# Two fp32-split feed-forwards on one core: high and low halves of the activations in one moving operand, and earlier norm diagonals

## The reference

```
# first block
h = rmsnorm(x, norm_mix_g);  proj = h @ w_in          # then RG-LRU, mLSTM, stick-breaking attention
x = x + merged @ w_o
hf = rmsnorm(x, norm_ffn_g)
gate, up = split(hf @ w_ffn_in)                        # 1024 -> 2 x 2816
x = x + (silu(gate) * up) @ w_ffn_out                  # 2816 -> 1024
x = rmsnorm(x, final_norm_g)
# second block
h = rms_norm(x, pre_mix_g)                             # mixer: spatial gating, MoBA attention, conv
x = x + rms_norm(concat(ya, yb, yc) @ w_out, post_mix_g)
m = rms_norm(mem, mem_g)                               # cross-attention on 256 memory tokens, w_xq, w_xkv, w_xo
h = rms_norm(x, pre_ffn_g)
f = square(relu(h @ w_ff1)) @ w_ff2                    # 1024 -> 4096 -> 1024
x = x + rms_norm(f, post_ffn_g)
```

## Time and profile before

| | us |
|---|---|
| median of three runs | 799.4 |
| lowest, highest | 798.67, 800.1 |
| the profiled execution, whole | 800.34 |
| its span in the profile | 798.6 |

### The profile page before, as it was taken

The page is one execution under the profiler, slowest core; times in us unless marked ns, Lnnn a source line. Parts: engine busy times, 40 slices in busy tenths (PEclk is TensorE's granted clock), DMA queues, the critical chain, the costliest instruction groups (busy, mean ns, idle before and its releaser), DMA issues.

```text
span 798.6 us, 11574 instructions
## 1 busy us (share of the span) xinstructions
PE 773.1 (97%) x4939; PEld 700.4 (88%) x4939; DVE 488.8 (61%) x528; ACT 387.9 (49%) x474; POOL 74.7 (9%) x87
## 2 busy tenths in 40 slices
PE   8999999989999999999969999999999999999996
PEld 8989887868999999999969888789988999999995
DVE  4555955486665556555655999776546655455543
ACT  6277466543553344343533478556345444444341
POOL 2000004020000000000214233020002000000001
PEclk9999999999999999999989999999999999999999
DMA  8455463436465654665534544446324655555431
GB/s 294 133 194 209 135 234 112 179 132 211 131 206 192 195 174 158 192 215 179 190 122 160 158 158 159 158 158 238 105 93 137 204 186 199 181 189 174 161 140 53
DMA packets 73940, 135.73 MB, mean 170 GB/s; under 512 B 4363, under 2 KB 28833, under 8 KB 73889
## 3 DMA queue, kind: packets, MB, share of 16 engines
q1 hardware_dynamic: 72080, 130.80, 49.0%
q10 hardware_dynamic: 1808, 4.19, 1.6%
HBM read 133.93 MB, written 1.05 MB: 169 GB/s over the span
## 4 chain that ended last, share of the span: by engine, by line
PE 89%; DVE 4%; ACT 3%; issue 1%; POOL 1%; DMA 0%; ACTq 0%; DVEq 0%
PE bank L1720 88%; DVE low L1175 2%; ACT arena L672 1%; PE bank L1807 1%; ACT high L672 1%; POOL arena L595 1%; ACT xn L672 0%; DVE arena L1376 0%; DMA vec_rows<-in_norm_mix_g_dram 0%; DVE x L1545 0%; ACT act_h L672 0%; DVE act_l L1224 0%; DVE arena L1467 0%; DVE arena L1358 0%; POOL var L524 0%
## 5 line engine op out<-in xcount | busy, mean ns | idle before, releaser
L1175 DVE TENSOR_TENSOR low<-raw,high 128x2048 fp32r<-128x2048 f32 (+1 forms) x118 | 266.2, 2279 | 142.0 <-ACT high L672 141.1
L672 ACT ACTIVATE high<-raw 128x2048 fp32r<-128x2048 f32 (+1 forms) x124 | 233.9, 1899 | 143.1 <-PE bank L1720 140.6
L1720 PE MATMUL bank<-act_h,low 128*128 128x256 f32 x864 | 246.5, 285 | 3.0 <-DVE act_l L1224 3.0
L1720 PE MATMUL bank<-act_h,high 128*128 128x256 f32 x864 | 245.7, 284 | 0.0
L1720 PE MATMUL bank<-act_l,high 128*128 128x256 f32 x864 | 245.6, 284 | 0.0
L1720 PEld LDWEIGHTS bank<-act_h,low 128*128 128x128 f32 x864 | 166.7, 193 | 4.2 <-issue 3.4
L1720 PEld LDWEIGHTS bank<-act_l,high 128*128 128x128 f32 x864 | 166.6, 193 | 0.7
L1720 PEld LDWEIGHTS bank<-act_h,high 128*128 128x128 f32 x864 | 166.6, 193 | 0.0
L1720 PE MATMUL bank<-high,act_l 128*128 128x512 f32 (+1 forms) x264 | 103.0, 390 | 2.8 <-DVE arena L1376 1.6
L1720 PE MATMUL bank<-high,hid_l 128*128 128x512 f32 x264 | 103.7, 393 | 0.0
L1720 PE MATMUL bank<-low,hid_h 128*128 128x512 f32 x264 | 103.0, 390 | 0.0
(11 more groups left out here) (180 smaller groups left out, 669.6 us busy)
## 6 DMA issues: line engine op xcount, KB each, us to landing
raw<-in_w_ff_dram SPq DMA_DIRECT2D x32, 1024.0 KB, 5.3
raw<-in_w_in_dram SPq DMA_DIRECT2D x30, 1024.0 KB, 5.4
raw<-in_w_ffn_in_dram SPq DMA_DIRECT2D x44, 512.0 KB, 4.8
raw<-in_w_ffn_out_dram SPq DMA_DIRECT2D x11, 1024.0 KB, 6.6
raw<-in_w_xkv_dram SPq DMA_DIRECT2D x8, 1024.0 KB, 5.1
raw<-in_w_o_dram SPq DMA_DIRECT2D x4, 1024.0 KB, 5.1
raw<-in_w_out_dram SPq DMA_DIRECT2D x4, 1024.0 KB, 5.1
raw<-in_w_xq_dram SPq DMA_DIRECT2D x4, 1024.0 KB, 5.1
```

The source lines that it names most:

```text
L672: return act.activation(dst, src, func, **k)
L1175: tt(part(low, g), part(raw, g), f32(part(high, g)), SUB).then_inc(sem.low_by_dve, 1)
L1720: return pe.matmul(dst, lhs, rhs, start=start, stop=stop, skip_group_check=loose)
```

## The change

`act_h` and `act_l` become one tile `act_hl` [128, 4, 2, 512], in which for each pair of row tiles the 512 numbers of the high part stand ahead of the 512 of the low part. For a row tile the high and the low 256 columns can be taken as one moving operand of two pieces (`both_of`).

A new mode "S" is used for the up products of both feed-forwards from c = 2 on. For a row tile and a channel tile it issues two matmuls: high weights by both halves of x, 512 columns, into a whole bank, and low weights by the high half, 256 columns, into the first half of the bank. So a chunk uses all four banks 0 to 3, which are now one PSUM tensor `wide`. ScalarE copies the second halves of the banks to SBUF (`hidden_low`, two copies of 512 columns that read two banks each), VectorE adds the first halves (`hidden_sum`, twice), and the chains go on from the sums; in the second feed-forward the ReLU becomes part of VectorE's multiply. TensorE waits for both sums of the chunk before (`hid_sum`) ahead of an up product.

At the seam VectorE makes the diagonals of norm 2 before `ahead_of(("kv", 0), "C")` and only the low quarters behind it, and ScalarE's `norm_split(2)` waits for one kv group less.

```
             if is_mem:
                 return hid_h[kt // 4][:, kt % 4, :], hid_l[kt // 4][:, kt % 4, :]
-            return act_h[:, kt, :], act_l[:, kt, :]
+            k = slice(kt % 2 * T, (kt % 2 + 1) * T)
+            return act_hl[:, kt // 2, 0, k], act_hl[:, kt // 2, 1, k]
+        def both_of(kt):
+            return act_hl[:, kt // 2, :, kt % 2 * T:(kt % 2 + 1) * T]
+        def wide_of(b, low_part):
+            return wide[:, 2 * b:2 * b + 2, low_part * T:(low_part + 1) * T]
...
-                self.pairs += {"W": 2, "F": 0}.get(mode, 1)
+                self.pairs += {"W": 2, "S": 2, "F": 0}.get(mode, 1)
...          # ScalarE
-                        act.wait_ge(sem.w_used, me.used - (n == 4))
+                        act.wait_ge(sem.w_used, me.used - (n in (2, 4)))
...
+            def hidden_low():
+                act.wait_ge(sem.w_used, me.used)
+                for b in range(2):
+                    f(in2(h_low[b]), wide_of(b, 1), ACT.Copy).then_inc(sem.hid_low, 1)
             def hidden1(c):
+                if c >= 2:
+                    hidden_low()
                 act.wait_ge(sem.hid_g, me.seen("hid_g"))
...
             def hidden2(c):
+                if c >= 2:
+                    hidden_low()
+                    for b in range(2):
+                        act.wait_ge(sem.hid_a, me.seen("hid_a", 1))
+                        f(flat(hid_h[c % 2][:, 2 * b:2 * b + 2, :]), (h_val, h_tmp)[b], ACT.Copy).then_inc(sem.hid_h, 1)
+                    return
...          # VectorE
+            def hidden_sum(b):
+                dve.wait_ge(sem.hid_low, me.seen("hid_low"))
+                tt(in2(h_low[b]), wide_of(b, 0), in2(h_low[b]), ADD).then_inc(sem.hid_sum, 1)
+                dve.wait_ge(sem.hid_sum, me.seen("hid_sum"))
             def hidden1(c):
-                dve.wait_ge(sem.w_used, me.used)
-                b0, b1 = me.pair()
-                tt(in2(h_tmp), in2(b0[:, :]), rep_2(), MUL).then_inc(sem.hid_g, 1)
+                if c >= 2:
+                    hidden_sum(0)
+                    gate, up = h_low
+                else:
+                    dve.wait_ge(sem.w_used, me.used)
+                    gate, up = (b[:, :] for b in me.pair())
+                tt(in2(h_tmp), in2(gate), rep_2(), MUL).then_inc(sem.hid_g, 1)
+                if c >= 2:
+                    hidden_sum(1)
                 dve.wait_ge(sem.hid_t, me.seen("hid_t"))
...
             def hidden2(c):
+                if c >= 2:
+                    value = h_val, h_tmp
+                    for b in range(2):
+                        hidden_sum(b)
+                    for b in range(2):
+                        stt(value[b], h_low[b], 0.0, h_low[b], MAX, MUL).then_inc(sem.hid_a, 1)
+                    for b in range(2):
+                        dve.wait_ge(sem.hid_h, me.seen("hid_h"))
+                        hl = flat(hid_l[c % 2][:, 2 * b:2 * b + 2, :])
+                        tt(hl, value[b], f32(flat(hid_h[c % 2][:, 2 * b:2 * b + 2, :])), SUB).then_inc(sem.hid_hl, 1)
+                        dve.wait_ge(sem.hid_hl, me.seen("hid_hl"))
+                    return
...
             final_norm()
+            norm_diag(2)
             ahead_of(("kv", 0), "C")
-            norm(2)
+            norm_split(2)
...          # TensorE, products
+                        elif mode == "S":
+                            for i in (2 * t, 2 * t + 1):
+                                ch = slice(i * P, (i + 1) * P)
+                                mm(bank[i][:, :], wh[:, j, ch], both_of(kt), s0, False)
+                                ins = mm(bank[i][:, 0:T], wl[:, j, ch], in_h, False, s1)
...
-                    if c >= 2:
-                        pe.wait_ge(sem.hid_a, c - 1)
-                    products(("up1", c), "C", fresh=c == 0, at=(2, turn_bottom) if c == 0 else None)
+                    if c == 2:
+                        pe.wait_ge(sem.hid_a, 2)
+                    elif c > 2:
+                        pe.wait_ge(sem.hid_sum, 2 * (c - 2))
+                    products(("up1", c), "S" if c >= 2 else "C", fresh=c == 0, at=(2, turn_bottom) if c == 0 else None)
...
-                    if c >= 2:
-                        pe.wait_ge(sem.hid_a, F1 // 256 + 2 * (c - 1))
-                    products(("up2", c), "C", fresh=c == 0)
+                    if c == 2:
+                        pe.wait_ge(sem.hid_a, n1 + 4)
+                    elif c > 2:
+                        pe.wait_ge(sem.hid_sum, 2 * (n1 - 2) + 2 * (c - 2))
+                    products(("up2", c), "S" if c >= 2 else "C", fresh=c == 0)
```

More of the change, by code:

```diff
@@ L142, in __init__ @@
         self.hid_hl = new("hid_hl")
+        self.hid_low = new("hid_low")
+        self.hid_sum = new("hid_sum")
         self.hid_t = new("hid_t")
@@ L349, in two_blocks @@
         h_val = carve(2 * T)
+        h_low = [carve(2 * T) for _ in range(2)]
         top[0] = 0
@@ L376, in two_blocks @@
         x_q = carve(KD, T)
-        bank = [ctx.enter_context(nc.psum_tensor(f"bank{i}", [P, NB], F32)) for i in range(8)]
+        wide = ctx.enter_context(nc.psum_tensor("wide", [P, 4, NB], F32))
+        bank = [wide[:, i, :] for i in range(4)]
+        bank += [ctx.enter_context(nc.psum_tensor(f"bank{i}", [P, NB], F32)) for i in range(4, 8)]
         sem = Semaphores(lambda name: ctx.enter_context(nc.semaphore(name)))
@@ L408, in split_of @@
                 return hid_h[kt // 4][:, kt % 4, :], hid_l[kt // 4][:, kt % 4, :]
-            return act_h[:, kt, :], act_l[:, kt, :]
+            k = slice(kt % 2 * T, (kt % 2 + 1) * T)
[4 more added lines that the diff above has]
+            return wide[:, 2 * b:2 * b + 2, low_part * T:(low_part + 1) * T]
         def branch_of(b):
-            return (hid1_h[b], hid1_l[b]) if b < 2 else (act_h[:, 4:6, :], act_l[:, 4:6, :])
+            return (hid1_h[b], hid1_l[b]) if b < 2 else (in2(act_hl[:, 2, 0, :]), in2(act_hl[:, 2, 1, :]))
         def hidden_of(c, first_ffn):
@@ L886, in turn_merged @@
                     act.wait_ge(sem.turned, me.seen("turned"))
-                    f(flat(act_h[:, 2 * q:2 * q + 2, :]), bank[4 + q][:, :], ACT.Copy, scale=0.5)\
+                    f(act_hl[:, q, 0, :], bank[4 + q][:, :], ACT.Copy, scale=0.5)\
                         .then_inc(sem.act_h, 1)
+            def hidden_low():
+                act.wait_ge(sem.w_used, me.used)
+                for b in range(2):
+                    f(in2(h_low[b]), wide_of(b, 1), ACT.Copy).then_inc(sem.hid_low, 1)
             def hidden1(c):
+                if c >= 2:
+                    hidden_low()
                 act.wait_ge(sem.hid_g, me.seen("hid_g"))
@@ L1008, in x_out @@
                     act.wait_ge(sem.x_o, me.seen("x_o"))
-                    f(flat(act_h[:, 2 * q:2 * q + 2, :]), bank[4 + q][:, :], ACT.Copy).then_inc(sem.act_h, 1)
+                    f(act_hl[:, q, 0, :], bank[4 + q][:, :], ACT.Copy).then_inc(sem.act_h, 1)
             def ahead_of(key, mode, hold=False):
@@ L1081, in _ @@
                 if c < n1:
-                    ahead_of(("up1", c), "C")
+                    ahead_of(("up1", c), "S" if c >= 2 else "C")
                     if c == 0:
@@ L1151, in _ @@
                 if c < n2:
-                    ahead_of(("up2", c), "C")
+                    ahead_of(("up2", c), "S" if c >= 2 else "C")
                     hidden2(c)
@@ L1387, in low_of_bank @@
                 dve.wait_ge(sem.act_h, me.seen("act_h"))
-                stt(flat(act_l[:, 2 * q:2 * q + 2, :]), (b or bank[4 + q])[:, :], scale,
-                    f32(flat(act_h[:, 2 * q:2 * q + 2, :])), MUL, SUB).then_inc(sem.act_hl, 1)
+                stt(act_hl[:, q, 1, :], (b or bank[4 + q])[:, :], scale,
+                    f32(act_hl[:, q, 0, :]), MUL, SUB).then_inc(sem.act_hl, 1)
             def turn_merged(c):
@@ L1427, in hidden1 @@
                 dve.wait_ge(sem.dve_step, me.step())
-                stt(h_val, h_tmp, 0.5, b1[:, :], MUL, MUL).then_inc(sem.hid_a, 1)
+                stt(h_val, h_tmp, 0.5, up, MUL, MUL).then_inc(sem.hid_a, 1)
                 dve.wait_ge(sem.hid_h, me.seen("hid_h"))
```

9 lines of the change are left out of this document (4 added, 5 removed).

## The result

The kernel after the change takes 788.9 us (787.8 to 789.6) against 799.3 us before: ratio 0.9869, interval 0.9851 to 0.9886, so by the ratio 10.5 us less (9.1 to 11.9), where 785.0 was forecast from 799.4, 14.4 less. The sign held, and so did the range of 8 in 10 (782.5 to 790.5); the forecast's own range (783.3 to 786.5) did not, since the gain forecast was 4 us too large. The profiled execution took 787.8 us with a span of 786.0.

What follows compares the result with a forecast made beforehand. TensorE, busy 97% of the span, was taken as the bound. Products 6.2 us plus seam 8.2 us made 14.4 us off the 799.4 median: 785.0 us, own range 783.3 to 786.5, 8-in-10 range 782.5 to 790.5.

Steps and rivals of the forecast that it cites:

- The size of the products' gain: Up products from c = 2, both feed-forwards: 480 matmuls saved at 0.013 us each, 6.2 us.
- wide matmuls spaced over 0.235: Sign in the up chunks that the forecast is wrong; 0.2265 us spacing was expected.
- The bound I gave: Extra cost of the two-piece operand in up products: from nothing to one fixed part per wide matmul, 6.2 us.
- The rule of the Trainium skill: Up products: warm spacing of N / 2.4 GHz plus 2.5 ns, so 480 fewer matmuls return an estimated 1.2 us.
- The handover of the banks: Between up chunks: sums finish at 3.0 us into the down chunk, TensorE needs the banks at 5.47, no wait.
- T: Start of the down chunk between two up chunks, from which the helpers' times are counted; 5.47 us long in the first feed-forward.
- The wait ahead of the last down chunk: At c = 10, no up chunk stands between, so TensorE stalls once for hid_l, 0.45 us.
- The seam: Between the two blocks: earlier diagonals and quarters give 6.6 us, the vanished later low clock 1.6, together 8.2 us.
- Passed on: Stage behind the seam: starts from this point on all engines, so the whole shift was taken as kept.
- the one that I gave 0.03: Rival, products: part of 0.0133 us goes with something else, perhaps weight buffer change between widths; 1.2 us saved, 790.0; chance 0.03.
- the products gain nothing: Rival, up products: the two-piece operand costs what the fixed part saved, little or no gain; 791.2 us, chance 0.05.
- the 1.4 us of longer chain at the seam: Hidden chain of c = 10 ends later by one copy and one sum, moving everything up to rstd by 1.4 us.

Runs made afterwards that it cites:

- by weight group: Kernel after the change, with the 16 wide matmuls of each weight group issued first, then its 16 narrow ones; 786.1 us, one execution.
- the one with the other half of the bank: Kernel after with x laid out in one piece per row tile and the narrow matmul adding into the second half of the bank; 789.2 us, timed once.

## Why the prediction was right, and where it was not

- **The size of the products' gain** is the step that failed: "480 x 0.013 = 6.2 us". The fixed part of 0.0133 us was read from streams of one width, and it is there: with the widths in groups a chunk takes 11.11 us, 0.02 from my 11.09. But mode S alternates, and a wide and a narrow matmul in turn cost 6 ns more a pair. The term measured 2.8 us, some 6 ns for each of the 480. The sign of being wrong that I had named, wide matmuls spaced over 0.235, was there, if only just: 0.23 and 0.24 in the rows, with 0.11 and 0.12 behind the narrow ones. The bound I gave, up to one fixed part for each wide matmul, held the cost; I had taken zero, and laid the risk to the two pieces, which cost nothing. The rows had a hint that I passed over: the down chunk after the narrow matmuls takes 5.47 for 24, 0.2279 each, where 0.2265 is the spacing further on the earlier trace rows.
- **The rule of the Trainium skill**, by which an estimated 1.2 us would come back ("TensorE: Matmul & The Clock Gate", "Back-to-back issue gap", 2.5 ns beside the columns, which the page gives for a matmul by itself). Here the fixed part is 13 ns in streams of one width, and the 480 saved returned 2.8 us in this order and 6.1 by weight group, so the measurements decide against its figure for these fp32r matmuls, each with its own weights.
- **The handover of the banks** was right: no wait on hid_sum, sums over at T + 2.85 (forecast 3.0), chain at T + 5.83 (5.8), subtraction from T + 7.0 (7.0). The wait ahead of the last down chunk was there: its matmul comes 0.60 after the one ahead instead of 0.23, 0.37 us (forecast 0.45).
- **The seam** was right in size and in its parts: 8.4 us for 8.2; diagonals ready 20.6 us after the down chunk as worked out, their products 3.49 us (3.5), zc after 27.72 us (28.0), a wait of 1.26 left (1.6), both low clocks gone. Of this, 6.88 came ahead of zc, 1.69 of it the clock of the diagonal products, and 1.51 from the later clock. Some luck is in how close it came: the kv subtractions began 0.3 us later than worked out (22.29 us after the down chunk, not 21.98) and took 4.49 us where I had carried over 4.93, and the two nearly cancel.
- **Passed on**: the stage behind gave nothing back, 220.51 us against 222.02, as taken.
- **The rivals.** None came as written. Nearest in mechanism was the one that I gave 0.03, that part of the 0.0133 us goes with the change between two widths and a saved matmul returns a fraction: it returned some 0.006 us, not the fifth (0.0027) that I had priced, and it was the order of the widths, not the weight tiles. The time lay between the forecast and "the products gain nothing". I had counted the 1.4 us of longer chain at the seam, but never set it against mode S: net it is worth 2.8 us in its rounds less 1.7 at the seam. By the timed runs the seam's order alone gives 9.0 us of the 10.9 that both give, and mode S alone could not be told from no change.

## What to carry to other kernels

A cost per matmul read from a uniform stream holds for uniform streams: with the matmuls of one width put together, here by weight group, nearly the whole of it came back (6.1 of 6.2 us). Work added to a helper chain was free in the loop, where other work covered it, and cost its full length once at the loop's end, where the next stage hangs on the chain. Before tuning a loop by hundreds of nanoseconds a round, look at the seams: here one reordered pair of small operations gave three times as much.

## What the runs showed of the hardware

- Matmuls of 512 and 256 columns in turn took 6 ns a pair more than the two spacings (0.3528 against 0.3464); with two of each the excess was 1.6 ns a pair (11.14 us a chunk), with 16 of each under 1 ns (11.11). Which part of TensorE it comes from was not tried.
- A moving operand in two pieces of 256 columns, 2 KB apart, ran as one in one piece (11.29 and 11.29 to 11.30 us), and which half of the bank was written (11.29), or a change of bank with each matmul (11.11 against a sum of spacings of 11.09), made no difference.
- At the seam the clock fell to 1.2 GHz for a stretch of the diagonal products only in the two kernels in which TensorE had stood still for 4.67 or 5.68 us ahead of them, and in both it fell once more, for some 3.4 us, in the product behind; with idle times of 1.02 to 1.46 us ahead of zc it stayed full. Whether the second fall follows from the first, or from the 1.93 us idle ahead of zc that both kernels have, no run separates.
- The two kv subtractions took 4.93 or 4.94 us in three of the eleven traces in which they stand side by side, and 4.49 or 4.50 in eight. In the three, a GpSimd operation on 512 columns (`affine_select`) began 1.89 to 2.09 us after the pair, while the first subtraction ran, and took 0.70 to 0.90 us; in the eight it began 2.21 to 3.07 us after, when the second ran, and took 1.93 to 2.79 us. The kernel after, then the one with the other half of the bank:

```profile
400.60 2.35 POOL L613 TENSOR_SCALAR_AFFINE_SELECT arena<-arena 128x512 f32<-128x512 f32 x1 [4.66 <-DMA arena<-in_w_s_dram]
...
398.93 4.93 DVE L1201 TENSOR_TENSOR low<-raw,high 128x2048 fp32r<-128x2048 f32 x2 [1.70 <-ACT high L685]
401.02 0.70 POOL L613 TENSOR_SCALAR_AFFINE_SELECT arena<-arena 128x512 f32<-128x512 f32 x1 [4.11 <-DMA arena<-in_w_s_dram]
```

  It reads as if the two engines took turns there, each operation waiting for the other engine's; 0.44 us of the wait ahead of zc hangs on when that GpSimd operation begins, and its row shows it released by a DMA. No experiment tried it.
- Executions of one kernel differ by up to 3 us (798.17 to 801.04 in 17 of the kernel before), and in two traces of the kernel after the difference lies in work that the change does not touch. In the second profile of the kernel after, the first down chunk begins at 226.86 instead of 224.56: 0.8 us come in the first dozen microseconds, and 1.5 from a stretch of low clock in the first mixer that the first profile does not have, although TensorE ran the same thin matmuls ahead of it in both (eight of 4 rows in 2.0 us):

```profile
74.00:80.00 6.00, 6.00 (x23) 4.80 (x22) 4.80 (x11) 5.43 (x11) 1.48 (x2) 0.79 0.21 76
```

  That is why parts are compared here from marks inside the traces, and totals from several executions.
